# Ten more projection units per layer as split products in the second scan, their weights' low parts partly on GpSimd

## What is computed

```python
u = _rmsnorm(h, norm_mix_g[l])
(s_z, s_xbc, s_dt, g_q, g_f, g_i, g_g, m_q, m_k, m_v, m_i, m_f, m_o, gates) = _split(u @ w_in[l], IN_SIZES)
y_ssd = _ssd_branch(...)                     # first scan
y_hg = _hgrn2_branch(g_q, g_f, g_i, g_g, ...)   # second scan
y_ml = _mlstm_branch(m_q, m_k, m_v, m_i, m_f, m_o, ...)
gate = jax.nn.sigmoid(gates.reshape(n_b, n_s, N_BRANCH, D_MODEL))
merged = (gate[:, :, 0] * (y_ssd @ w_br_ssd[l]) + gate[:, :, 1] * (y_hg @ w_br_hg[l])
          + gate[:, :, 2] * (y_ml @ w_br_ml[l]))
h = h + merged @ w_out[l]
```

## Time and profile before

| | |
|---|---|
| median of 3 runs | 2211.87 us (2209.24 to 2212.95) |
| profiled execution, its own time | 2209.24 us |
| its span, first to last instruction | 2207.2 us |
| PE busy / PEld busy | 2024.6 us (92%) / 1719.5 us |
| DVE / ACT / POOL busy | 1202.5 / 878.0 / 30.8 us |
| mean granted TensorE clock | 0.962 |
| layer 0's second scan (steps 2 to 23, `gh`, `gh+1`) | about 226 to 430 us |
| layer 1's second scan | up to 1218 us |

### The profile page before, as it was taken

One profiled execution on the slowest core, in us unless ns is written; L12 is line 12 of the kernel. 1 busy time (PEld: TensorE's weight loads), 2 busy tenths in 40 slices (PEclk: granted clock), 3 DMA queues, 4 the chain that ended last, 5 costly groups with the idle time before them and its releaser, 6 DMA issues.

```text
span 2207.2 us, 47710 instructions
## 1 busy us (share of the span) xinstructions
PE 2024.6 (92%) x20606; PEld 1719.5 (78%) x20606; DVE 1202.5 (54%) x2113; ACT 878.0 (40%) x1057; POOL 30.8 (1%) x61
## 2 busy tenths in 40 slices
PE   8999999999999999999999999999999777767776
PEld 7998858889999989988588989999887543333333
DVE  5887756388677557886663796875433200000001
ACT  5555533474565455546343554564412200000001
POOL 0000000000000000000000000000000000000000
PEclk9999999999999999999999999999999888788888
DMA  6565333444445544553434444555574799999997
GB/s 228 177 215 180 123 146 135 164 161 172 172 178 194 204 159 173 204 194 129 160 117 149 176 168 163 186 184 198 213 305 156 301 420 422 422 422 423 422 422 303
DMA packets 71496, 498.80 MB, mean 226 GB/s; under 512 B 8384, under 2 KB 8512, under 8 KB 12976
## 3 DMA queue, kind: packets, MB, share of 16 engines
q1 hardware_dynamic: 66384, 480.75, 57.2%
q0 software_dynamic: 4384, 14.75, 2.0%
q10 hardware_dynamic: 576, 1.05, 0.2%
HBM read 495.37 MB, written 1.15 MB: 225 GB/s over the span
## 4 chain that ended last, share of the span: by engine, by line
PE 70%; DMA 14%; DVE 6%; ACT 5%; SPq 3%; issue 2%; DVEq 0%; ACTq 0%
PE bank L877 25%; PE bank L882 13%; PE bank L887 9%; DMA ring<-stream 8%; DMA arena<-stream 6%; SPq L727 3%; PE bank L1119 3%; PE bank L820 2%; PE bank L865 2%; PE bank L832 2%; PE bank L1374 2%; PE bank L913 1%; PE bank L1222 1%; PE bank L870 1%; PE bank L1095 1%
## 5 line engine op out<-in xcount | busy, mean ns | idle before, releaser
L887 PE MATMUL bank<-u,ring 128*128 128x256 f32 x1152 | 256.1, 381 | 0.0
L2321 DVE TENSOR_TENSOR ring_r<-ring,weights_and_u_split 128x2048 fp32r<-128x2048 f32 x88 | 201.5, 2291 | 91.0 <-ACT weights_and_u_split L1741 87.3
L887 PEld LDWEIGHTS bank<-u,ring 128*128 128x128 f32 x1152 | 216.9, 190 | 30.2 <-issue 0.8
L2655 DVE COPY arena<-bank 128x128 f32<-128x128 f32 x32 | 9.3, 291 | 401.7 <-PE bank L1392 401.7
L882 PE MATMUL bank<-weights_and_u_split,ring_r 128*128 128x256 f32 x1592 | 208.9, 283 | 0.0
L877 PE MATMUL bank<-weights_and_u_split,hidden_and_weights_high 128*128 128x256 f32 x1600 | 202.2, 284 | 0.0
L1741 ACT ACTIVATE weights_and_u_split<-ring 128x2048 fp32r<-128x2048 f32 x88 | 167.9, 1909 | 81.7 <-PE bank L882 49.4
L877 PEld LDWEIGHTS bank<-weights_and_u_split,hidden_and_weights_high 128*128 128x128 f32 x1600 | 195.4, 192 | 4.8 <-issue 4.3
L882 PEld LDWEIGHTS bank<-weights_and_u_split,ring_r 128*128 128x128 f32 x1592 | 199.0, 192 | 0.0
L2321 DVE TENSOR_TENSOR ring_r<-ring,hidden_and_weights_high 128x2048 fp32r<-128x2048 f32 x60 | 137.0, 2286 | 34.2 <-ACT hidden_and_weights_high L1741 34.2
L1374 PE MATMUL bank<-ring,arena 128*32 128x256 f32 x1008 | 90.4, 490 | 58.3 <-DMA ring<-stream 58.3
(11 more groups left out here) (396 smaller groups left out, 3453.4 us busy)
## 6 DMA issues: line engine op xcount, KB each, us to landing
ring<-stream SPq DMA_DIRECT2D x328, 1024.0 KB, 4.9
arena<-stream SPq DMA_DIRECT2D x128, 1024.0 KB, 26.3
arena<-rows_scratch POOLq DMA_DIRECT2D x48, 256.0 KB, 4.0
h<-x_d ACTq DMA_DIRECT2D x4, 256.0 KB, 5.3
out<-arena SPq DMA_DIRECT2D x2, 512.0 KB, 2.6
con<-con_d SPq DMA_DIRECT2D x1, 976.5 KB, 14.0
arena<-con_d POOLq DMA_DIRECT2D x1, 848.0 KB, 7.1
par<-par_d POOLq DMA_DIRECT2D x2, 422.0 KB, 4.7
```

The source lines that it names most:

```text
L887: mm = pe.matmul(bank[:, c * S:(c + 1) * S], w[:, k, c * P:(c + 1) * P], x[:, k, :], start=(k == 0), stop=(k == KC - 1))
L2321: tt(ring_r[:, POS[k] % RING, :], w, high(k).bitcast(F32), ALU.subtract).then_inc(wlo_ok.sem, 1)
```

## The change

The four `mo`, four `gs` and the first two `gh` units of each layer become split units: `SCAN`, put between `EARLY` and `MID` in `SPLIT`. Their high parts are ACT copies in the step before the unit; those of `mo` and `gs` have their low parts made by GpSimd, between its two groups of row transfers, and those of `gh` and `gh+1` by DVE. High parts lie in areas that the scan no longer needs (two halves of `HF`, `MERGED`, later 42 and 0). The split of `u` moves forward: its high part (`u_high`, ACT) to step 10, into two halves of `HK` (`scan_u`), its low part (`u_low`, DVE, over `u`) to the head of step 12, behind the last plain unit that reads `u` (`mv`). Behind `gh+1` ACT now copies the high part of `u` from there to `UHI2`, and DVE has nothing left to do at that place but to wait for it.

```diff
-SPLIT = EARLY + MID + [n for n, kind in enumerate(KINDS) if kind in ("up", "down", "pleg")]
+SCAN = [n for n, kind in enumerate(KINDS) if kind in ("mo", "gs")] + [OF["gh"], OF["gh"] + 1]
+SPLIT = EARLY + SCAN + MID + [n for n, kind in enumerate(KINDS) if kind in ("up", "down", "pleg")]
...
+        WSCAN = (HF, 122, HF, 122, HF, HF, HF, HF, 42, 0)
+        WHI2, UHI2, YHHI, YMHI, MGHI = (42, 74, 0), 16, (114, 116, 118, 96), 24, 114
...
         for i in range(2, 24):
+            if i in (17, 19, 21):
+                sched.append(("hi", gs + i - 15))
+            elif i == 23:
+                sched.append(("hi", gh))
+            elif 11 <= i <= 15:
+                sched.append(("hi", mo + i - 11 if i < 15 else gs))
+            if i == 12:
+                sched.append(("u_low", 0))
             sched.append(("products", mq + i))
...
+            if i == 23:
+                sched.append(("lo", gh))
+            if i == 10:
+                sched.append(("u_high", 0))
             sched.append(("read", mq + i))
...
-        sched += [("products", gh), ("products", gh + 1), ("mlA", 0), ("mlA", 1), ("split", gh + 2), ("read", gh),
+        sched += [("products", gh), ("split", gh + 1), ("products", gh + 1), ("mlA", 0), ("mlA", 1), ("split", gh + 2), ("read", gh),
                   ("xsplit", (1, range(4))), ("hi", gh + 3), ("read", gh + 1)]
...
+                for n in SCAN[:8]:
+                    pool.wait_ge(whi_ok.sem, whi_ok.at(lay, NTH_SPLIT[n] + 1))
+                    slot = POS[n] % RING
+                    pool.tensor_tensor(scan_high_or_low(n, ring_r[:, slot, :]), scan_high_or_low(n, ring[:, slot, :]),
+                                       high(n).bitcast(F32), ALU.subtract).then_inc(wlo_ok.sem, 1)
                 pool.wait_ge(hcp.sem, hcp.at(lay, HSTEPS))
                 pool.wait_ge(ho_ok.sem, ho_ok.at(lay, 4))
...
+                elif kind == "u_high":
+                    act.wait_ge(hqk.sem, hqk.at(lay, 9))
+                    for j in range(4):
+                        act.activation(scan_u(2 * j, 2).rearrange("p c s -> p (c s)"), u[:, 2 * j:2 * j + 2, :].rearrange("p c s -> p (c s)"),
+                                       ACT.Copy).then_inc(uhi_ok.sem, 1)
...
                     if k == 1:
-                        dve.wait_ge(unit_done.sem, unit_done.at(lay, POS[OF["gh"] + 1] + 1))
+                        dve.wait_ge(uhi_ok.sem, uhi_ok.at(lay, 12))
+                        return
...
+                elif kind == "u_low":
+                    dve.wait_ge(unit_done.sem, unit_done.at(lay, POS[last("mv")] + 1))
+                    for j in range(4):
+                        dve.wait_ge(uhi_ok.sem, uhi_ok.at(lay, 4 + j + 1))
+                        x, low = (t[:, 2 * j:2 * j + 2, :].rearrange("p c s -> p (c s)") for t in (u, u_r))
+                        ins = tt(low, x, scan_u(2 * j, 2).bitcast(F32).rearrange("p c s -> p (c s)"), ALU.subtract)
+                    ins.then_inc(ulo_ok.sem, 1)
```

More of the change, by code:

```diff
@@ L263, in program @@
         as_r, at = {}, 0
-        for name, first, n in (("hidden_low", 0, 50), ("weights_and_u_split", 58, 40), ("hidden_and_weights_high", 102, 28)):
+        for name, first, n in (("hidden_low", 0, 42), ("scan_weights_high", 42, 16), ("weights_and_u_split", 58, 40), ("hidden_and_weights_high", 102, 28)):
             if first > at:
@@ L347, in high, with scan_high_or_low @@
         def high(n):
+            if n in SCAN and high_at(n) == HF and n < OF["gh"]:
+                return halves_r(HF)
             return flat_r(high_at(n), KC)
+        def scan_high_or_low(n, x):
+            return x.rearrange("p (d n) -> p d n", d=2) if n in SCAN and high_at(n) == HF and n < OF["gh"] else x
         def high_at(n):
@@ L356, in high_at @@
             i -= len(EARLY)
+            if i < len(SCAN):
+                return WSCAN[i]
+            i -= len(SCAN)
             return WHI2[i % 3] if i < len(MID) else WHI[(i - len(MID)) % 3]
@@ L769, in _ @@
             LATE = {OF["bm"]: 4, OF["out"]: 6, OF["pleg"]: 6}
-            FIRST = {EARLY[0]: 0, MID[0]: 1, OF["bh"]: 2, OF["bm"]: 3, OF["out"]: 4, OF["up"]: 5, OF["pleg"]: 6}
+            FIRST = {EARLY[0]: 0, OF["mo"]: 1, MID[0]: 2, OF["bh"]: 3, OF["bm"]: 4, OF["out"]: 5, OF["up"]: 6, OF["pleg"]: 7}
+            LOWS = {EARLY[0]: 1, OF["mo"]: 2, MID[0]: 2, OF["bh"]: 3, OF["bm"]: 4, OF["out"]: 5, OF["up"]: 6, OF["pleg"]: 7}
             def unit(lay, n):
@@ L836, in unit @@
                     ks = min(KC, FC - KC * sub) if kind == "down" else KC
-                    whi, wlo = (x.rearrange("p (k m) -> p k m", k=KC) for x in (high(n), ring_r[:, POS[n] % RING, :]))
+                    wlo = ring_r[:, POS[n] % RING, :].rearrange("p (k m) -> p k m", k=KC)
+                    if scan_high_or_low(n, slot) is slot:
+                        wide = high(n).rearrange("p (k m) -> p k m", k=KC)
+                        whi = [wide[:, k, :] for k in range(KC)]
+                    else:
+                        wide = high(n).rearrange("p d (k m) -> p d k m", k=4)
+                        whi = [wide[:, k // 4, k % 4, :] for k in range(KC)]
+                    wlo = [wlo[:, k, :] for k in range(KC)]
                     if kind == "up":
@@ L848, in unit @@
                         xhi, xlo = chunks_r(UHI, KC), chunks_r(HLO, KC)
+                    elif n in SCAN:
+                        yhi = [scan_u(k, 1)[:, 0, :] for k in range(KC)]
+                        xhi, xlo = None, u_r
                     elif kind in ("gh", "gm"):
@@ L1554, in unit @@
                     at = dst + 2 * j
+                    if n == OF["gh"] + 1:
+                        act.wait_ge(uhi_ok.sem, uhi_ok.at(lay, 12))
                     if kind == "mo" and j == 0:
@@ L1732, in item @@
                         act.wait_ge(unit_done.sem, unit_done.at(lay, POS[m] + 1))
-                    if i == len(EARLY):
-                        act.wait_ge(unit_done.sem, unit_done.at(lay, POS[last("bs")] + 1))
-                    elif i == len(EARLY) + 1:
+                    if k == OF["gh"]:
+                        act.wait_ge(unit_done.sem, unit_done.at(lay, POS[OF["gs"] + 6] + 1))
+                    elif k == OF["gh"] + 1:
+                        act.wait_ge(unit_done.sem, unit_done.at(lay, POS[OF["bs"] + 6] + 1))
+                    elif k == OF["gh"] + 3:
                         act.wait_ge(yh_fin.sem, yh_fin.at(lay, 1))
-                    elif i == len(EARLY) + 2:
-                        act.wait_ge(yh_fin.sem, yh_fin.at(lay, 1))
-                    elif i == len(EARLY) + len(MID):
+                    elif k == OF["up"]:
                         act.wait_ge(unit_done.sem, unit_done.at(lay, POS[last("bh")] + 1))
-                    act.activation(high(k), ring[:, POS[k] % RING, :], ACT.Copy).then_inc(whi_ok.sem, 1)
+                    act.activation(high(k), scan_high_or_low(k, ring[:, POS[k] % RING, :]), ACT.Copy).then_inc(whi_ok.sem, 1)
+                elif kind == "u_high":
[3 more added lines that the diff above has]
+                                       ACT.Copy).then_inc(uhi_ok.sem, 1)
                 elif kind == "hsplit":
@@ L2024, in item @@
                     if k == 1:
-                        dve.wait_ge(unit_done.sem, unit_done.at(lay, POS[OF["gh"] + 1] + 1))
+                        dve.wait_ge(uhi_ok.sem, uhi_ok.at(lay, 12))
+                        return
                     for j in pieces:
-                        dve.wait_ge(uhi_ok.sem, uhi_ok.at(lay, 4 * (k + k // 5) + j + 1))
+                        dve.wait_ge(uhi_ok.sem, uhi_ok.at(lay, 4 * (k + 1 + k // 5) + j + 1))
                         if k == 5:
                             x, low = h[:, 2 * j:2 * j + 2, :].rearrange("p c s -> p (c s)"), flat_r(HLO + 2 * j, 2)
-                        elif k == 1:
-                            x, low = (t[:, 2 * j:2 * j + 2, :].rearrange("p c s -> p (c s)") for t in (u, u_r))
                         else:
@@ L2320, in item @@
                     w = ring[:, POS[k] % RING, :]
-                    tt(ring_r[:, POS[k] % RING, :], w, high(k).bitcast(F32), ALU.subtract).then_inc(wlo_ok.sem, 1)
+                    tt(scan_high_or_low(k, ring_r[:, POS[k] % RING, :]), scan_high_or_low(k, w), high(k).bitcast(F32), ALU.subtract)\
+                        .then_inc(wlo_ok.sem, 1)
                 elif kind == "hsplit":
```

23 lines of the change are left out of this document (13 added, 10 removed).

## The result

The changed kernel takes 2223.54 us (median of 4, 2222.58 to 2226.34) against 2211.24 us before (median of 4, 2209.24 to 2212.95): ratio 1.0058, 95% interval 1.0041 to 1.0075. It is 12.3 us slower; forecast were 20 us less, in a range that ends at 2223. The direction is the one that the first rival gave, and so is what the profile shows.

A forecast was written before the change was run, and what follows sets the result against it. PE's own work bounds the scan, DVE's chain having 2.05 us of slack. Net 10.7 - 0.6 = 10.1 us per layer, 20.2 in all, off the median 2211.87 gives 2191.7, given as 2191.5; range 2187 to 2223.

The forecast's parts named there:

- Plain against split: Units of `mo`, `gs`, `gh`, `gh+1`: a split unit takes 5.94 us against 7.11 between levels; gain 10.7 us per layer.
- Weight copies and u's low part: ACT's ten weight copies (1.91 us) beside PE's units, DVE's low part of `u` (2.5 us) before step 12: cost 0.
- Behind bs: Low parts of `gh` and `gh+1` on DVE delay ACT's copies into `UHI2`: PE stalls 0.6 us (0 to 1.0).
- GpSimd's subtractions: Beside DVE's chain in the second scan: each takes 4.5 us (between 2.29 and 6.63), cost 0.
- H: Time for which GpSimd's subtraction holds DVE in a step; 4.5 us taken, 2.29 and 6.63 as bounds.
- Rival 1: GpSimd's subtraction stops DVE's chain in four steps per layer: net +3.8 us per layer, 2219 us in all; chance 0.38.
- the decision point: Hold of DVE, 3.6 us, from which four collisions per layer cost more than the 10.1 us gained.
- Rivals 2 and 3: 2: GpSimd excludes DVE but waits for its chain, 2208 us, chance 0.14. 3: late low parts, 2202 us; with mishaps 0.08.

The follow-up runs named there:

- the run with 16 columns: Changed kernel with GpSimd's subtractions on 16 of 2048 columns, PE's third group taking the high part of the weights: 2190.26 us.
- the fill: Changed kernel with GpSimd filling the 2048 columns with zeros instead of subtracting, PE's third group taking the high part: 2197.6 us (one run).
- The half subtraction: Changed kernel with GpSimd subtracting 1024 of 2048 columns, PE's third group taking the high part for the other four chunks: 2203.40 us.
- the copy: Changed kernel with GpSimd copying the 2048 columns onto themselves instead of subtracting, PE's third group taking the high part: 2196.2 us (one run).

## Why the prediction was wrong

- **Plain against split: right.** A split unit between levels took 5.94 us, the step 6.63. From `mo` 0's start to `gh+2`'s the run with 16 columns needs 420.36 - 317.54 = 102.82 us, against 430.78 - 316.75 = 114.03 before. That is 11.2 less, of which the first group of `gh+2` gives back 2.93 - 2.26 = 0.67: 10.5 per layer for the 10.1 predicted. That the total agrees as well, 2190.26 us for 2191.5, is partly luck: that execution needs 3.0 us less than the one before between `gh+2` of layer 1 and the last norm, and 3.8 more in the norm; neither was forecast, and they nearly cancel.
- **Weight copies and u's low part: right.** ACT's copies took 1.90 us and delayed nothing; `u_low` ran at 311.20 for 2.50 us, ahead of the unit.
- **Behind bs: right,** 0.67 us of stall for 0.6.
- **GpSimd's subtractions: the step that failed.** Their length was right (mean 4585 ns for 4.5 us); "I take 4.5, the middle, and cost it at 0" was wrong. The cost is that of a held DVE: with H = 4.4 us and a slack of 6.63 - 5.81 = 0.82 (0.88 predicted), 3.6 us in a step (10.24 against 6.63), and 117.95 - 102.82 = 15.1 us in layer 0, where I had put nothing. I took line 751's transfers as weak evidence that the two do not exclude each other. But such a transfer reads `rows_scratch`, which isn't in SBUF, and the fill shows that a GpSimd instruction without an input from SBUF holds nothing: that row could not bear on the question. The Trainium skill (SBUF — State Buffer, Who interferes with whom) states the exclusion for exactly these operands, and that a GpSimd instruction that only writes is exempt. The traces agree on both (5.08 us beside the subtraction, 0.69 beside the fill). A stated rule stood against a row of another kind, and I gave the rule too small a chance.
- **Rival 1: right in mechanism and place.** It gave +3.8 us per layer, stall behind `bs` included; layer 0 lost 3.9 up to `gh+2` and 0.67 in its first group, 4.6, of which 1.5 is a fall of the clock that the rival did not count (below). Its 2219 missed 4.5 us, and the last norm alone lost 4.8. The half subtraction (H = 2.23, below 3.6) came out faster than before, as its formula has it; between 2.23 and 4.4 the decision point is not tested.
- **Rivals 2 and 3: not seen.** GpSimd did not wait for the end of the chain by itself (it starts 0.07 us ahead of DVE's third instruction), and PE waits for POOL nowhere in the scan. Made to wait, it gave 2214 and a step of 9.56 us; the rival said 2208 and 9.0 to 9.5.
- **Clock.** Rival 1 named a fall only for holds of 6.63 us; it came at 4.4 already. In the held steps it cost nothing, since the slow groups lay inside DVE's hold; in the step of `gs` 0, which has no hold, the unit took 361.44 - 354.04 = 7.40 us instead of 5.94. Layer 1 lost 5.35 us from `mo` 0 to `gh+2`, 1.4 more than layer 0. Its rows put that behind the fourth wait, where the level and the next group take 1.98 and 1.83 us (1.15 and 1.22 in layer 0), at a granted clock of 0.54 against 1.00. That the clock makes this 1.4 is read from rows, not tested.
- **Open:** the last norm (above), and 1.5 us that came between `gh+2` of layer 1 (8.16 later) and that norm (9.65 later). In the twelve profiled executions this stretch takes between 974.4 and 980.5 us (977.4 before), one profile each, and nothing here ties that spread to a change. So a few microseconds of a total say little of the scan; the lengths from `mo` 0 to `gh+2` say more (102.82 and 102.85 us with 16 columns and with the fill).

## What to carry to other kernels

Before work is moved to GpSimd, list what VectorE does in the same microseconds: an elementwise GpSimd instruction that reads SBUF stopped VectorE's instructions between SBUF operands until its own end here, and GpSimd needed twice VectorE's time (4.59 us against 2.29), so the same work on VectorE itself was cheaper where the two met (2197.5 us, against 2223.5). Ask where in the dependent loop the work falls: the 2.28 us on VectorE cost 7.41 - 6.63 = 0.78 per step beside PE's level, and a hold of 2.23 inside the loop cost 8.04 - 6.63 = 1.41. A row about another kind of instruction (a transfer) is no evidence against such a hold.

## What the runs showed of the hardware that I had not expected

- **Which instructions exclude each other.** GpSimd's subtraction (4.6 us) and its copy (1.90 us) hold VectorE, its fill (1.81 us) does not. Held are VectorE's two-input instructions and also its copy from SBUF to SBUF (0.76 to 4.62 us for two); the predicated copy out of PSUM (0.44 us) is not. The one that starts later waits: GpSimd's copy took 2.42 us behind a VectorE instruction.
- **PE often comes back from a wait at half pace.** In layer 0, behind 4.03, 2.05 and 2.58 us of idle time the next eight matmuls took 2.08 us, and 1.75 or 1.32 the eight after; behind 1.33 and 1.52 us they took 1.22 as ever. It is not idle time alone: behind 2.28 us ahead of `gs` 1 they took 1.22 too, and behind the same 2.63 us ahead of a level in the first half of the scan the next unit took 7.13 us in the kernel before, 7.65 with the copy and 8.83 with the fill. The granted clock says what the pace is: 0.50 over the eight matmuls from 343.82 to 345.69 in the changed kernel, 1.00 from 347.28 on, that is 1.2 and 2.4 GHz.
- **Gaps on issue.** From 200 us on PE's program has five to seven gaps of over 0.5 us in which it waits for nothing but issue, 8 to 13 us in all, in each of the twelve versions; they move when instructions are added ahead of them. A change of 5 us far from an edit can be this.
